# Delta net chunks: the state times the keys, then the inverse applied to what is left of the values

## The reference, cut to what matters

```python
k_beta = k * beta[..., None]
lower = where(strict, einsum('bhnid,bhnjd->bhnij', k_beta, k) * decay, 0.0)
rhs = concatenate([v * beta[..., None], k_beta * exp(gc)[..., None]], axis=-1)
sol = triangular_solve(lower + eye, rhs, ...)      # u | w
...
def step(state, inp):
    v_new = u_c - einsum('bhck,bhkv->bhcv', w_c, state)
    o_c = einsum('bhck,bhkv->bhcv', q_c, state) + einsum('bhij,bhjv->bhiv', a_c, v_new)
    state = state * gl[..., None, None] + einsum('bhck,bhcv->bhkv', k_c, v_new)
```

## Time and profile before

| | us |
|---|---|
| median of three runs | 3335.62 |
| the profiled execution | 3333.01 |
| its span | 3331.2 |
| PE busy in the span | 3100.7 (93%) |
| DVE / ACT / POOL busy | 1553.6 / 1002.6 / 433.9 |
| heads 0 to 7 of the delta net | from about 82 to 748 |
| granted TensorE clock, mean | 0.973 |

### The profile page before, as it was taken

The page is one execution under the profiler, slowest core; times in us unless marked ns, Lnnn a source line. Parts: engine busy times, 40 slices in busy tenths (PEclk is TensorE's granted clock), DMA queues, the critical chain, the costliest instruction groups (busy, mean ns, idle before and its releaser), DMA issues. The chain is left out here.

```text
span 3331.2 us, 36380 instructions
## 1 busy us (share of the span) xinstructions
PE 3100.7 (93%) x15051; PEld 2518.8 (76%) x15051; DVE 1553.6 (47%) x1912; ACT 1002.6 (30%) x1440; POOL 433.9 (13%) x343
## 2 busy tenths in 40 slices
PE   7899999979999999999688998989879999999998
PEld 5788888867788888887565666877767788888886
DVE  7566656652664543333456761654463322222223
ACT  5555555542211111112423332222222211111111
POOL 4222223221000000001100000332131000000001
PEclk9999999999999999999888999999999999999999
DMA  3111111112233331112110001010012111111111
GB/s 124 33 45 45 45 45 45 45 64 102 89 108 120 114 97 49 50 46 87 42 51 5 9 10 41 20 38 32 26 58 100 42 47 50 46 51 45 51 43 59
DMA packets 77237, 184.78 MB, mean 55 GB/s; under 512 B 7056, under 2 KB 29072, under 8 KB 77072
## 3 DMA queue, kind: packets, MB, share of 16 engines
q1 hardware_dynamic: 77072, 182.44, 17.5%
HBM read 163.87 MB, written 15.79 MB: 54 GB/s over the span
## 5 line engine op out<-in xcount | busy, mean ns | idle before, releaser
L497 PE MATMUL ps<-b 128*128 128x512 f32 x5928 | 1474.4, 399 | 46.4 <-DVE b L1316 15.0
L497 PEld LDWEIGHTS ps<-b 128*128 128x128 f32 x5928 | 1091.3, 190 | 259.4 <-issue 26.8
L1512 PE MATMUL ps<-b 128*128 128x512 f32 x2592 | 608.5, 395 | 0.5 <-DVE b L1643 0.5
L1512 PEld LDWEIGHTS ps<-b 128*128 128x128 f32 x2592 | 485.1, 187 | 119.0 <-DVE b L1643 1.0
L486 DVE TENSOR_TENSOR b<-b 128x1024 fp32r<-128x1024 f32 (+1 forms) x206 | 254.7, 1237 | 326.9 <-ACT b L478 319.9
L2806 PE MATMUL ps<-b 128*128 128x512 f32 (+1 forms) x1584 | 363.9, 386 | 37.1 <-DVE b L1866 14.4
L478 ACT ACTIVATE b<-b 128x1024 fp32r<-128x1024 f32 (+1 forms) x206 | 215.1, 1045 | 562.7 <-PE ps L1512 463.8
L2806 PEld LDWEIGHTS ps<-b 128*128 128x128 f32 x1584 | 283.6, 197 | 94.8 <-issue 42.7
L1381 POOL TENSOR_TENSOR b<-b 128x1024 f32<-128x1024 f32 x24 | 57.5, 2397 | 1642.7 <-ACT b L1387 1642.3
L1558 ACT ACTIVATE b<-ps 128x1024 f32<-128x1024 f32 x54 | 55.4, 1025 | 389.2 <-PE ps L497 389.2
L2152 PE MATMUL ps<-b 128*128 128x512 f32 x320 | 163.0, 592 | 0.0
(11 more groups left out here) (291 smaller groups left out, 3297.1 us busy)
## 6 DMA issues: line engine op xcount, KB each, us to landing
b<-in_down SPq DMA_DIRECT2D x52, 512.0 KB, 3.6
b<-in_mod SPq DMA_DIRECT2D x96, 256.0 KB, 2.7
b<-in_gu SPq DMA_DIRECT2D x44, 512.0 KB, 3.6
b<-scratch SPq DMA_DIRECT2D x38, 512.0 KB, 4.4
b<-in_dn_in SPq DMA_DIRECT2D x32, 512.0 KB, 4.9
b<-in_up SPq DMA_DIRECT2D x32, 512.0 KB, 3.7
b<-in_win SPq DMA_DIRECT2D x26, 512.0 KB, 4.0
scratch<-b SPq DMA_DIRECT2D x18, 512.0 KB, 3.0
```

The lines of the kernel that those rows point to most:

```text
L497: ins = e.matmul(ps[:, c], w, h[:, k, c], start=first and k == 0 and i == 0, stop=last and k == KT - 1 and i == 2)
L1512: ins = e.matmul(ps[:, c], w, u[:, at[k], c], start=k == 0 and p == 0, stop=k == n - 1 and p == 2)
```

## The change

The product of inverse and decayed keys ahead of the chunks goes away: L916 on PE, the eviction L1039 on ACT, `kbe` on POOL. In chunk n (from 1 on) PE now multiplies the keys with the state into a PSUM tile U (L936), DVE makes `un` = exp(gc) U - vb (new, L1179), and PE applies the inverse to that (L941); DVE scales by minus p into `vn` (L1185). So five matmuls stand in a chunk as before, but they form three steps with an engine change each (L936, L941, L948) where there were two. Fills are moved too: the second fill after the product of half 1 in each level is dropped, and the chunk gets a third fill, between L938 and L941. ACT's two fills of the chunk become three to match. The lines of after that answer to those of before: L876, L894, L901, L910 are the same; L1143, L1146, L1036, L1028 are L1132, L1135, L1028, L1020; L941 and L945 are L941 and L936; L949, L954, L957 are L938, L948, L949; L1197 is L1193; L2705, L2717, L2720, L2752 are L2699, L2711, L2714, L2746; L1049, L1054 are L1037, L1042.

```diff
-            yield 1 + f
+            yield 1
 ...
-        e.wait_ge(*A.at("xt", h, 6, f))
-        e.wait_ge(*G.at("kbe", h, f))
-        for n in ns:
-            ins = e.matmul(blk(D1, n), blk(d["kbe"], n), blk(x1, n), start=True, stop=True)
-        ins.then_inc(*P.up("w", h, f))
-        yield
 ...
-            if n:
-                e.wait_ge(*V.at("vn", h, n - 1))
-            ins = e.matmul(V1, blk(d["x1"], n), blk(d["vb"], n), start=True, stop=n == 0)
             if n:
-                e.wait_ge(*A.at("wt", h, 1))
                 e.wait_ge(*V.at("st", h, n - 1))
-                ins = e.matmul(V1, blk(wt, n), st[n % 2], start=False, stop=True)
-            ins.then_inc(*P.up("v", h, n))
-            if n:
+                e.matmul(U, blk(k, n), st[n % 2], start=True, stop=True).then_inc(*P.up("u", h, n))
                 e.wait_ge(*G.at("qd", h, n // 4))
                 e.matmul(blk(D1, n), blk(qd, n), st[n % 2], start=True, stop=False)
+                side.fill(1)
+                e.wait_ge(*V.at("u", h, n))
+            e.matmul(V1, blk(d["x1"], n), un[n % 2] if n else blk(d["vb"], n), start=True, stop=True).then_inc(*P.up("v", h, n))
             side.fill(1)
             e.wait_ge(*V.at("vn", h, n))
 ...
-            side.fill(1)
+            side.fill(2 if n else 1)
 ...
+            if n:
+                e.wait_ge(*P.at("u", h, n))
+                e.scalar_tensor_tensor(out=un[n % 2], in0=U, scalar=self.egc[:, n, h:h + 1], in1=blk(d["vb"], n),
+                                       op0=ALU.mult, op1=ALU.subtract).then_inc(*V.up("u", h, n))
+                side.fill(1)
             e.wait_ge(*P.at("v", h, n))
-            e.tensor_scalar(vn[n % 2], V1, sm["p"][:, n:n + 1], None, ALU.mult).then_inc(*V.up("vn", h, n))
+            e.tensor_scalar(vn[n % 2], V1, sm["np" if n else "p"][:, n:n + 1], None, ALU.mult).then_inc(*V.up("vn", h, n))
 ...
-            for f in range(2):
-                e.wait_ge(*A.at("kt", h, f))
-                by_token(h, f, "kbe", d["kbe"], d["kt"], self.egc[:, :, h])
```

More of the change, by code:

```diff
@@ L379, in memory @@
                 self.d_x = sb([128, KT, T], ctx=first)
-            self.d |= {n: big() for n in ("y", "lt", "at", "kt", "kbe", "kd", "vb", "x1")}
+            self.d |= {n: big() for n in ("y", "lt", "at", "kt", "kd", "vb", "x1")}
             self.d |= {n: sb([128, 512], ctx=ph) for n in ("m0", "m1", "t", "xc", "xs")}
-            self.d_vn = [sb([128, 128], ctx=ph) for _ in range(2)]
+            self.d_vn, self.d_u = ([sb([128, 128], ctx=ph) for _ in range(2)] for _ in range(2))
             self.d_st = [sb([128, 128], ctx=ph) for _ in range(2)]
@@ L922, in pe_delta_rest @@
         D0, D1 = self.psl[2], self.psl[3]
-        d, vn, st = self.d, self.d_vn, self.d_st
-        qd, wt = self.d_set[h % 2][0:2]
-        V1, S2 = D0[:, 0:128], D0[:, 512:640]
+        d, vn, un, st = self.d, self.d_vn, self.d_u, self.d_st
+        qd, k = self.d_set[h % 2][0:2]
+        V1, U, S2 = D0[:, 0:128], D0[:, 128:256], D0[:, 512:640]
         def turn(f):
@@ L936, in pe_delta_rest @@
                 turn(0)
-            if n:
-                e.wait_ge(*V.at("vn", h, n - 1))
             if n % 4 == 0:
                 e.wait_ge(*G.at("vb", h, n // 4))
-            ins = e.matmul(V1, blk(d["x1"], n), blk(d["vb"], n), start=True, stop=n == 0)
+            if n == 0:
+                e.wait_ge(*A.at("xt", h, 6, 0))
             if n:
-                e.wait_ge(*A.at("wt", h, 1))
                 e.wait_ge(*V.at("st", h, n - 1))
-                ins = e.matmul(V1, blk(wt, n), st[n % 2], start=False, stop=True)
-            ins.then_inc(*P.up("v", h, n))
-            if n:
+                e.matmul(U, blk(k, n), st[n % 2], start=True, stop=True).then_inc(*P.up("u", h, n))
                 e.wait_ge(*G.at("qd", h, n // 4))
                 e.matmul(blk(D1, n), blk(qd, n), st[n % 2], start=True, stop=False)
+                side.fill(1)
+                e.wait_ge(*V.at("u", h, n))
+            e.matmul(V1, blk(d["x1"], n), un[n % 2] if n else blk(d["vb"], n), start=True, stop=True).then_inc(*P.up("v", h, n))
             side.fill(1)
             e.wait_ge(*V.at("vn", h, n))
+            if n == 0:
+                e.wait_ge(*A.at("xt", h, 6, 1))
             if n < 7:
@@ L954, in pe_delta_rest @@
                 e.matmul(S2, blk(d["kd"], n), vn[n % 2], start=True, stop=True).then_inc(*P.up("s", h, n))
-            if n == 0:
-                e.wait_ge(*A.at("wt", h, 1))
             e.matmul(blk(D1, n), blk(d["at"], n), vn[n % 2], start=n == 0, stop=True).then_inc(*P.up("o", h, n))
@@ L1037, in act_delta_half @@
             yield 0
-        e.wait_ge(*P.at("w", h, f))
-        e.activation(self.d_set[h % 2][1][:, hs], D1[:, hs], ACT.Copy, scale=-1.0).then_inc(*A.up("wt", h, f))
-        yield
     def act_delta_rest(self, e, h, side):
@@ L1074, in dve_delta @@
         P, A, V, G = self.dn
+        e.wait_ge(*A.at("egc"))
         side = DeltaSide(DveDelta(self, e))
@@ L1154, in dve_delta_rest @@
         d, sm, vn, st = self.d, self.d_sm, self.d_vn, self.d_st
-        V1, S2 = D0[:, 0:128], D0[:, 512:640]
+        V1, U, S2 = D0[:, 0:128], D0[:, 128:256], D0[:, 512:640]
+        un = self.d_u
         half = lambda f: (slice(512 * f, 512 * f + 512), slice(4 * f, 4 * f + 4))
@@ L1185, in dve_delta_rest @@
                 side.until(h, 3)
+            if n % 4 == 0:
+                e.wait_ge(*G.at("vb", h, n // 4))
+            if n:
[3 more added lines that the diff above has]
+                side.fill(1)
             e.wait_ge(*P.at("v", h, n))
@@ L1259, in pool_delta @@
                     for f in range(2):
+                        e.wait_ge(*A.at("kt", h, f))
                         by_token(h, f, "kd", d["kd"], d["kt"], self.kdf[:, :, h])
```

## The result

The changed kernel took 3357.14 us (median of four runs, 3354.65 to 3359.81) beside 3335.76 of the kernel before (four runs): a ratio of 1.0063 with a 95% interval of 1.0045 to 1.008. It is slower by 21 us. The forecast was 3362 us, 28 us more between the profiled executions; the result is inside the range of 3343 to 3378.

What follows compares the result with a forecast made beforehand. PE was taken to bound the delta net, busy 78.4 of 82.0 us per head. Head 0 +2.7, six heads +23, last head +3.0, boundary -0.9 gave +28 us on 3333.0, forecast 3362 us, range 3343 to 3378.

Steps and rivals of the forecast that it cites:

- What goes: L916's eight products per head leave PE: 1.7 us per head, 13.7 in all, all on the path.
- (a): Level two: L876 of half 1 needs L1132, which stands behind L486 on DVE; 1.25 us of waiting per head.
- (b): Level three: it holds three taps on DVE beside its own work; 1.3 us of waiting per head.
- (c): Level six: L910 of half 1 needs the addition behind L486; 1.1 us of waiting per head.
- (d): Chunks 0 to 2, with the next head's k taps between DVE steps, and chunk 3: waits sum to 1.2 us.
- (f): Chunks 6 and 7, with three taps, L1159 and L1162: late `un`, `vn` and state, sum 1.4 us.
- (e): Chunk 5: `vn` stands on DVE behind L486, so L948 starts 2.4 us late, where the row had 0.95.
- the hand rule: Weight chain before: DVE's start at 325.16 plus 0.49 gives PE's next matmul at 325.65, as in the row.
- The last head and the end: Last head +3.0 us, the state's step 0.39 to 0.47 late in six chunks; between head 6 and 7 -0.9.
- Rival 1: The clock falls behind the 2.4 us gap of (e), some 1.5 us a head: 3372, twice a head 3382; chance 0.11.
- Rival 2: The third fill covers the chunk's third step, waiting stays near 3.6 us a head: 3319 us; chance 0.09.
- Rival 3: Chunk waits grow as in (e), but (a) to (c) do not; growth equals L916: 3335 us; chance 0.09.

Runs made afterwards that it cites:

- experiment 1: The kernel before without L916 and its copy L1039, the chunks using the keys in its place: 3323.17 us, 0.9953.
- Experiment 2: The kernel before, arithmetic untouched, with only the fills moved as the change moves them: 3345.1 us, 1.0018.
- experiment 7: The changed kernel with ACT's root of the first output half put behind the eviction and high part in chunk 5: 3350.99 us, 1.0042.
- experiments 2 to 4: Experiment 2, then the changed kernel with the fills of before, 3361.45 us, and the changed kernel with L941 fed from values instead of `un`, 3355.93 us.
- experiment 8: The changed kernel with L486 of k and v in the thirteenth fill, z's in the eighth, and next-head taps only in fills of four: 3321.78 us, 0.9955.
- experiment 5: The changed kernel with DVE's low part of the weights (L486) moved from a unit's first fill to its fourth, among the taps: 3387.04 us, 1.0139.
- experiment 6: The changed kernel with L486 in a unit's seventh or eighth fill, behind the taps, the head's first unit unchanged: 3341.75 us, 1.0013.

## Why the prediction came out right

The places and the direction were right; that the sum came so near is in part luck. The six middle heads were forecast 7.3 us too high. The last head and the end came out 3.8 us higher than forecast (+3.0 and +2.9 against +2.1 and 0), by a fall of the clock that the sum does not have. And the +2.7 up to head 1 was forecast as waiting in head 0, where PE's idle time rose by 0.1 us; the rest is the 0.8 ahead of that head and its slower clock.

**What goes: right.** 13.7 forecast; 14.4 measured in the total and 15.0 by the heads (experiment 1), so all of it was on the path.

**(a), (b), (c): right in place and size.** 1.25, 1.3 and 1.1 forecast; the idle times are 1.14, 1.42 and 1.05. Experiment 2 shows them without the new arithmetic. In (a) the working adds 0.40 behind L1132, where its own rule gives 0.33 for an operation of 0.28. The wait for ACT's copy ahead of L941, 0.25, did not come in the middle heads.

**(d), (f): somewhat too high.** Of 0.77 at `vn` in chunk 1, 0.50 came; of 0.8 at `un` in chunk 6, 0.65, and in heads 2 to 5 the slower clock just ahead of it covered it. The 0.14 in odd chunks came at L948, as in chunk 3 (due at 324.62 + 0.55, start at 325.31).

**(e): right.** 2.4 forecast. L948 was due at 331.39 + 0.55 = 331.94 and started at 334.18: 2.24 late, of which 2.08 are idle. The root's share of 0.7 was measured as 0.6 (2.08 against 1.5, experiment 7). One confirmation in the prediction was none: the hand rule "gives" 325.65 with a 0.49 that was read from that very row. With the 0.40 that (e) uses it gives 325.56.

**The sum of the waits mixed two measures.** My 8.9 us are delays from start to start; the 3.6 of before that I took off are idle time. A delay holds some 0.16 us in which the last matmul runs out (2.24 against 2.08). With 13 waits that is 2.1, so the forecast in idle time is 6.8, and head 1 has 84.59 - 77.66 = 6.9. The trace has only six waits there; the small ones of the forecast left no idle time that it shows. On the same measure the growth is 3.3, not 5.3. In return PE's busy time fell by 1.0 and not by 16 x 0.11 = 1.76: ends and restarts cost 0.76, where I had 0.3. So 3.3 - 1.0 = +2.3 a head at full clock, against +3.9 forecast.

**The last head and the end: too low.** The state's step is late by 0.22 to 0.48 of idle in the chunks (0.39 from start to start where it is 0.22, as worked out). The boundary gained 1.85, not 0.9. But L923 waited 2.78 us where L930 had 0.93, since the pieces had run out, and the output product behind took 5.49 us and not 3.02 at a clock of about 0.5: +2.4 that I had not seen. In experiment 2 the same two gaps stand ahead of this group and it takes the same 5.49 us, so this too comes with the moved fills.

**Rival 1 held in part.** The clock did fall behind (e) in heads 2 to 5, at a cost of 0.3 to 0.4 us each, and not in heads 1 and 6 with the same gap of 2.08. (Head 4 takes 0.65 more than heads 1 and 6, but 0.3 of that it also has in experiment 7, at a clock of 1.00.) I had priced it at 1.5. It also fell where rival 1 did not look, at the output product. The rule of the Trainium skill on idle gaps between bursts (TensorE: Matmul & The Clock Gate, Why this matters for your kernels) warns of such gaps, and these rows bear the warning out, but at gaps shorter than those it names; the size is from the rows. **Rival 2** is refuted by experiments 2 to 4 for the kernel as it is. What it claims, that a third fill covers the third step, is nearly so in experiment 8, and even there the step costs as much as L916 did, if L916 is worth there what it is in experiment 1. **Rival 3** failed at (a) to (c), which came in full.

Of the +1.3 a head between experiment 2 and the change, 1.0 stands in heads 1 and 6 at full clock; the rest is the clock where it fell. Why the clock falls behind one gap of 2.08 us and not behind the next stays open.

## What to carry to other kernels

Before an extra hand-over to another engine is traded for less work on the bounding one, price it from start to start, with the run-out of the product ahead (0.17) and the restart (0.10) beside the idle time; here that is 0.63 us a chunk uncovered and 0.2 to 0.3 well covered (the table's 1.8 over seven chunks), against 1.87 us once a head for the product. Then look at what stands in order on the other engine: moving the long VectorE operations into the stretches where TensorE has four matmuls to do brought 1.3%, while the change of arithmetic brought nothing. Such operations must be spread; putting the low part among the taps (experiment 5) cost 0.9%.

## What the hardware showed that I had not expected

The granted clock fell behind a gap of 2.08 us in four heads of six and not in the two others, with the same instructions around it; behind 1.5 us (experiment 7) it stayed at 1.00. The length of one gap does not decide it: in experiment 5 it fell behind two gaps of 1.48 and 1.16 us with six matmul records between (0.56 at 346 to 348 us), and in experiment 6 it stayed at 1.00 behind a single gap of 1.47 at the same place. It fell to about 0.5 behind two gaps of 2.78 and 1.44 us with only four short matmuls between, and not where they were 0.93 and 1.44.

A VectorE tap on 128x1024 takes 1.28 us alone and, in head 1, 1.83 and 1.66 while GpSimd works beside it (L1219 from 206.18 to 208.29, L1266 from 208.25 to 210.52); the tap of 205.66 still took 1.28, though L1219 started during it; the low part of the weights took 1.23 alone and 2.29 in experiment 5, beside L1266.
